# Which engine makes the low halves of the weight tiles between two sublayers

## The reference

```
def swiglu(h, wg, wu, wd):
    return (silu(h @ wg) * (h @ wu)) @ wd
def sandwich_in(h, m, sub, p):
    return rms_norm(h, p['norm_pre'][sub]) * (1 + m[:, 3*sub+1]) + m[:, 3*sub]
def sandwich_out(h, y, m, sub, p, weight):
    return h + weight * m[:, 3*sub+2] * rms_norm(y, p['norm_post'][sub])
def ffn_sub(h, m, sub, j, p):
    y = swiglu(sandwich_in(h, m, sub, p), p['w_gate'][j], p['w_up'][j], p['w_down'][j])
    return sandwich_out(h, y, m, sub, p, 0.5)
```

## Time and profile before

| | us |
|---|---|
| median of the runs | 3351.67 |
| profiled execution, its own time | 3364.72 |
| span of that execution | 3362.2 |
| TensorE busy | 3113.3 (93%) |
| VectorE busy | 1709.3 (51%) |
| ScalarE busy | 1017.1 (30%) |
| GpSimd busy | 281.9 (8%) |
| mean granted TensorE clock | 0.953 |

### The profile page before, as it was taken

One profiled execution on the slowest core, in us unless ns is written; L12 is line 12 of the kernel. 1 busy time (PEld: TensorE's weight loads), 2 busy tenths in 40 slices (PEclk: granted clock), 3 DMA queues, 4 the chain that ended last, 5 costly groups with the idle time before them and its releaser, 6 DMA issues.

```text
span 3362.2 us, 49317 instructions
## 1 busy us (share of the span) xinstructions
PE 3113.3 (93%) x17920; PEld 2858.8 (85%) x17920; DVE 1709.3 (51%) x3019; ACT 1017.1 (30%) x1714; POOL 281.9 (8%) x256
## 2 busy tenths in 40 slices
PE   7999999889898789999999899999988898789998
PEld 3999999879655688999998899999977655689997
DVE  3576565555235754355424666546456337544334
ACT  2312112443424433121123312112343425432223
POOL 2000000410000041000004100000230000310002
PEclk8999999989979899999999899999989899899999
DMA  5343344322100032243323344324331200333333
GB/s 190 111 139 113 113 125 125 103 70 57 53 1 1 1 100 72 60 125 114 99 63 94 93 115 137 112 88 123 106 88 57 60 1 1 92 95 96 94 92 108
DMA packets 454132, 293.19 MB, mean 87 GB/s; under 512 B 25974, under 2 KB 411356, under 8 KB 453980
## 3 DMA queue, kind: packets, MB, share of 16 engines
q1 hardware_dynamic: 453074, 288.02, 29.7%
q10 hardware_dynamic: 906, 3.18, 0.2%
HBM read 289.04 MB, written 2.10 MB: 87 GB/s over the span
## 4 chain that ended last, share of the span: by engine, by line
PE 81%; DVE 9%; issue 4%; ACT 4%; POOL 2%; DMA 0%; ACTq 0%; DVEq 0%; POOLq 0%
PE ps L1639 23%; PE ps L1641 23%; PE ps L1640 23%; PE ps L1976 2%; PE ps L1975 2%; PE ps L2048 2%; PE ps L2001 1%; DVE wsp L1127 1%; DVE hn L1215 1%; POOL scr L700 1%; ACT wsp L766 1%; PE ps L1988 1%; ACT hn L796 1%; DVE ps L1208 1%; PE ps L2033 1%
## 5 line engine op out<-in xcount | busy, mean ns | idle before, releaser
L1639 PE MATMUL ps<-hn,wsp 128*128 128x384 f32 (+1 forms) x3200 | 1059.6, 331 | 56.4 <-DVE hn L1215 34.9
L1640 PE MATMUL ps<-hn,wsp 128*128 128x384 f32 (+1 forms) x3200 | 1047.3, 327 | 0.0
L1641 PE MATMUL ps<-hn,wsp 128*128 128x384 f32 (+1 forms) x3200 | 1046.9, 327 | 0.0
L1127 DVE TENSOR_TENSOR wsp<-raw,wsp 128x1024 fp32r<-128x1024 f32 x376 | 467.4, 1245 | 580.0 <-ACT wsp L766 579.9
L1639 PEld LDWEIGHTS ps<-hn,wsp 128*128 128x128 f32 x3200 | 611.8, 191 | 76.8 <-DVE hn L1215 36.0
L1640 PEld LDWEIGHTS ps<-hn,wsp 128*128 128x128 f32 x3200 | 614.0, 192 | 0.0
L1641 PEld LDWEIGHTS ps<-hn,wsp 128*128 128x128 f32 x3200 | 612.9, 192 | 0.0
L766 ACT ACTIVATE wsp<-raw 128x1024 fp32r<-128x1024 f32 x408 | 428.0, 1051 | 533.7 <-PE ps L1641 533.5
L1639 PE MATMUL ps<-aT,wsp 128*128 128x384 f32 (+1 forms) x1408 | 460.4, 327 | 30.2 <-DVE aT L1306 19.4
L1641 PE MATMUL ps<-aT,wsp 128*128 128x384 f32 (+1 forms) x1408 | 456.3, 324 | 0.0
L1640 PE MATMUL ps<-aT,wsp 128*128 128x384 f32 (+1 forms) x1408 | 456.0, 324 | 0.0
(11 more groups left out here) (205 smaller groups left out, 3099.4 us busy)
## 6 DMA issues: line engine op xcount, KB each, us to landing
modw<-in_w_mod SPq DMA_DIRECT2D x144, 512.0 KB, 4.2
raw<-in_ffn_w_gate SPq DMA_DIRECT2D x192, 256.0 KB, 3.4
raw<-in_ffn_w_up SPq DMA_DIRECT2D x192, 256.0 KB, 4.2
raw<-in_ffn_w_down SPq DMA_DIRECT2D x64, 448.0 KB, 3.4
raw<-in_w_in SPq DMA_DIRECT2D x96, 256.0 KB, 3.1
raw<-in_ffn_w_down SPq DMA_DIRECT2D x64, 256.0 KB, 4.2
raw<-in_w_out SPq DMA_DIRECT2D x64, 256.0 KB, 3.1
raw<-in_ffn_w_down SPq DMA_DIRECT2D x64, 192.0 KB, 3.2
```

Source lines behind the costliest of these rows:

```text
L1127: dve.tensor_tensor(wsp[:, cs, 1, 0:width], raw[:, slot, 0:width], wsp[:, cs, 0, 0:width].bitcast(F32), ALU.subtract).then_inc(wlo_done, 1)
L1639: pe.matmul(dst, w(0), x(0), start=first, stop=False)
L1640: pe.matmul(dst, w(0), x(1), start=False, stop=False)
L1641: return pe.matmul(dst, w(1), x(0), start=False, stop=last)
```

## The change

`split_by_pool` returns False for every tile. So at the ends of the sublayers the low halves of down 1, 3, 6 and 7 and of head 0 and 1 are made by DVE, in `next_lo` of DVE's program, at the place in the step lists that is described above. POOL's `next_lo` never issues anything. The high halves, the loads, the counts of the semaphores and the lists stay as they are; DVE's extra wait on `wlo_done`, which it had behind a low half of POOL, goes.

```
     for l in range(L):
         for sub in range(3):
             i = t - CONV - last_tile0(l, sub) - KD
             if 0 <= i < KD:
-                return i in (1, 3, 6, 7)
+                return False
             i = t - CONV - first_tile0(l, sub)
             if 0 <= i < HEAD:
-                return i < HEAD - 2 and (l, sub) != (0, 0)
+                return False
     return False
```

## The result

The changed kernel took 3391.15 us (median of four runs, 3381.77 to 3393.65), the kernel before 3354.52 beside it: ratio 1.0107, 95% interval 1.0076 to 1.0138. Run once more on another occasion (experiment 4) it had a ratio of 1.0076, interval 1.0049 to 1.0103. So it is slower by some 25 to 37 us. The profiled executions, 3364.72 us before and 3393.65 after, differ by 28.9.

The account below looks back on a forecast made before the run. Taking the order of steps in sublayer boundaries, with VectorE pacing the pre steps, as the limit, it summed 16.6 + 3.7 - 1.3 = 19.0 us, plus 3.5 for the clock: 22.5 us slower, 3374 us; range 3354 to 3392.

Parts of the forecast that it names:

- Tail, down 1 to 5: Down 1 to down 5: ScalarE's squares wait for VectorE instead of GpSimd, ending at the same time; 0 us.
- Pre steps: Down 6 to pre 6: two low halves delay the chain VectorE paces; 2.7 us per boundary of 384.
- the reciprocal: Lead, head 0: VectorE's low half goes ahead of the reciprocal, making it 1.0 us late.
- Lead: Low half of head 1 holds back post 2, 4, 6, so GpSimd's adds start late; 1.45 us per boundary of 384.
- the boundary with halves of 256: Same two low halves in pre steps and lead, but shorter VectorE steps, so its tail wins a little; 3.7 us.
- Last boundary: Sixth boundary, only down 1 and 3: TensorE's waits for GpSimd shrink, post steps hold evacuations; -1.3 of 1.9 us.
- Clock: TensorE idles more in boundaries, so more time at the lower clock; 0.7 us for each of five, 3.5 us.
- Order of steps: All six boundaries before the clock: 16.6 + 3.7 - 1.3 = 19.0 us slower.
- A: Waits for ScalarE hide all but the second pre-step low half; lead loses nothing; 11 us slower, 3362 us; chance 0.24.
- B: GpSimd's chain was the limit, so freeing it speeds tails and lead; 26.5 us faster, 3325 us; chance 0.07.
- C: Clock falls further in five boundaries with TensorE on the path; 17.5 us on top of 19, 3388 us; chance 0.14.
- D: Nothing changes, all moved work lies within waits; 3352 us; chance 0.03.

Follow-up runs that it names:

- experiment 4: The changed kernel run once more, all 32 low halves on VectorE, against the kernel before: ratio 1.0076.
- experiment 1: Kernel before with only the low halves of down 1 and down 3 (12 of 32) moved to VectorE: no difference, interval -7 to +5 us.
- experiment 7: Kernel before with only down 1 and 3's low halves moved to VectorE, placed behind post 0 and post 4: 20.4 us faster.
- number 9: Changed kernel plus unused matrix products filling TensorE's waits before the mean of x half 0 and inside head 0: ratio 1.0024 to the kernel before.
- number 10: Kernel before plus unused matrix products filling its shorter TensorE waits before the mean of x half 0 and inside head 0: 14.5 us faster.
- Experiment 2: Kernel before with only the low halves of down 6 and down 7 (10 of 32) moved to VectorE: +15.2 us.
- experiment 5: Changed kernel with VectorE's low half of head 1 placed behind post 6 instead of ahead of post 2: ratio 1.0046 to the kernel before.
- filled pair: The changed kernel and the kernel before, each with unused products filling TensorE's waits (number 9 and number 10): medians 23.9 us apart.
- Experiment 3: Kernel before with only the low halves of head 0 and head 1 (10 of 32) moved to VectorE: 12.0 us slower.
- the parts: Three runs, each moving one group of low halves in the kernel before: down 1 and 3, down 6 and 7, head 0 and 1; sum 26.7 us.

## Why the prediction was right, and where its size was off

**Tail, down 1 to 5 (taken: 0; the stall changes its releaser).** Right. y0 to x0 moved by +0.7, +0.7, +0.1, +0.5 and, with halves of 256, -0.8 us; experiment 1 shows no difference, and experiment 7 shows what the low half ahead of the post step hides. Of the first +0.7, 0.17 us is there when PE starts the mean (656.41 - 2.13 = 654.28 for 654.11). The low half of down 3 ended at 646.43 - 2.13 = 644.30, near the 644.35 that the prediction gave for waiting out POOL's add in full, and not at its 644.1. The other 0.54 us is the mean itself, 1.41 us for 0.87 at a granted clock of 0.50 for 0.84.

**Pre steps (2.7 us) and the reciprocal (1.0).** Right: 2.79 us in the row above, and at a full clock x0 to y1 is 23.25 us in number 9 for 19.43 in number 10: 3.82, forecast 3.73. Experiment 2 gives +15.2 us for the pre steps of five boundaries. That the next three boundaries show the same rows within a few tenths was not so before the change: x0 to y1 was 21.8 twice, then 22.9 and 20.3.

**Lead (0.45 us behind the reciprocal, 1.45 in all).** The mechanism holds (4.32 us of standing still, experiment 5 takes it back), the size was too small. In the filled pair y1 to x1 is 18.2 us for 17.4 at halves of 384, 0.8 instead of 0.45. The step that was wrong is that with the reciprocal 1.0 us late head 1 would be only 0.5 late, because PE had columns of head 1 in hand. Head 1 came late in full. ACT's high half of head 1 starts 4.90 us behind the reciprocal in number 9 and 4.93 in number 10, and 7.21 us behind it both in the changed kernel and before in the first boundary (in the others of 384 it was 0.35, 0.24 and 0.0 us nearer after the change). What was to cover the delay shows as idle time of PE ahead of the spread, in number 10 and in number 9:

```profile
677.29 0.93 PE L1671 MATMUL ps<-cst,inv 128*128 128x128 f32 x6 [0.35 <-DVE inv L1186]
```

```profile
681.89 0.94 PE L1671 MATMUL ps<-cst,inv 128*128 128x128 f32 x6 [1.36 <-DVE inv L1186]
```

With halves of 256 the stretch grew by 2.2 us, and a second cause is added. The low half waits for ACT, and ACT for PE to end head 1, as the prediction had it, but PE ran head 1 at the lower clock. In the boundary with halves of 256, DVE's post 0 and ACT's high half of head 1, before and after:

```profile
2947.31 0.76 DVE L1234 TENSOR_TENSOR ps<-yM,ps 128x256 f32<-128x256 f32 x2 [0.80 <-PE ps L1671]
```

```profile
2949.85 1.06 ACT L766 ACTIVATE wsp<-raw 128x1024 fp32r<-128x1024 f32 x1 [0.54 <-PE ps L1641]
```

```profile
2976.39 0.76 DVE L1234 TENSOR_TENSOR ps<-yM,ps 128x256 f32<-128x256 f32 x2 [1.31 <-PE ps L1671]
```

```profile
2980.49 1.06 ACT L766 ACTIVATE wsp<-raw 128x1024 fp32r<-128x1024 f32 x1 [2.11 <-PE ps L1641]
```

From the one to the other it was 2.5 us and is 4.1. From the reciprocal to that high half, before and after, PE has the same 28 products, 3.29 us of work and then 5.36, and the granted clock is 1.00 and then 0.57:

```profile
2946.34:2949.85 3.51, 3.29 (x28) 3.29 (x29) 2.71 (x9) 0.81 (x3) 3.03 (x2) 1.00 0.06 15
```

```profile
2974.91:2980.49 5.58, 5.36 (x28) 5.36 (x29) 1.71 (x6) 0.81 (x2) 1.47 (x2) 0.57 0.33 94
```

The filling does not take this back: in number 9 the clock there is 0.66. Experiment 3, +12.0 for 7 to 10, points the same way.

**Last boundary (-1.3).** It won 2.9 us, 2.2 in the trace of number 4 and 2.0 between numbers 10 and 9: the two waits of 0.95 are gone, and the 0.6 taken for evacuations held back by the post steps was not there. Where the up to 1.0 us beyond 1.9 comes from stays open.

**Clock (3.5).** 3.6 by the difference of the filled and the unfilled pairs, and rather more: number 9 was at the lower level for 3.4 us in the fourth boundary in spite of the filling, and took 24.83 us from x0 to y1 there, for 23.25 in the first. In no boundary of number 10 is that so in this stretch.

```profile
2441.27:2466.10 24.83, 21.79 (x112) 19.56 (x111) 15.50 (x38) 9.65 (x22) 4.11 (x5) 0.93 0.26 64
```

That the clock was worth 14.5 us before the change (experiment 10) I had not seen.

**Sum.** Order of steps: forecast 19.0 including the last boundary. The traces of the filled pair have 25.6 - 2.0 = 23.6, the medians of numbers 9 and 10 have 23.9. Of the missing 4.6 us, 1.6 are the lead at halves of 384, 1.6 the fourth boundary as just said, and 1.5 the boundary with halves of 256 (5.2 for 3.7); the last boundary gives 0.7 back, and the rest is spread over small differences. With the clock the forecast was 22.5, and the traces without filling have 29.2 - 2.9 = 26.3. The first comparison's 36.6 us lies above that; the parts (26.7) and the repetition (25.4) lie on it. Why its four runs came out some 10 us higher than the seven of the repetition stays open; the intervals overlap between 1.0076 and 1.0103.

**The rivals.** A fell by experiments 2 and 3, which are slower by themselves. Its price did not follow from its condition either: with one low half of 1.2 us lost per boundary and nothing in the lead, 5 x 1.2 - 1.3 is 4.7 us and not 11. B was wrong about the change, and yet its source was real: 15.8 us lay in POOL's low halves of the tail, and number 7 got them with DVE's behind the post steps. C had the clock falling by 7 us more per boundary, and its price, 19 + 17.5 = 36.5 us, is the 36.6 of the first comparison; by the total alone C would have won, and that the median still lies in the range owes something to luck. Five boundaries did go from 113 to 157 us at the lower level, 8.8 each, but the filled pair shows that only 0.7 of it per boundary, or about 1 with the fourth, lengthened the path beyond the order, for 3.5 in C. D is excluded.

## What to carry to other kernels

Where engines walk through fixed lists, the price of an instruction moved to another engine is what stands behind it there, and behind the wait it brings, until the bounding engine gets its next input: here 0 us or 2.7 us for two instructions of 1.2, and a gain of 3.2 us per boundary when the two of 0 stood one step later. Follow the first piece of work behind the new wait, not the busy share; and if that wait leads back to TensorE, reckon it at the clock that TensorE has there. Count an engine's work as cover for a delay only if that work outlasts the delay: in the lead, with the waits filled, PE was through with it and stood idle for 1.36 us. A stall at the bounding engine is worth removing only if the replacement does not delay the same next input.

## What was not expected of the hardware

- Products without a use, put into TensorE's waits, made the kernel before 14.5 us faster (ratio 0.9957, 0.9939 to 0.9975), with nothing else changed: the granted clock from x0 to y1 rose from 0.81 to 1.00 in the first boundary.
- A low half of VectorE over an add of GpSimd took 1.55 us in the earlier trace rows and 1.71 us three times in the first tail of the changed kernel, for 1.23 alone. This is the row of the second of them:

```profile
644.72 1.71 DVE L1127 TENSOR_TENSOR wsp<-raw,wsp 128x1024 fp32r<-128x1024 f32 x1 [1.08 <-ACT wsp L766]
```

The best version run (12) keeps down 6, 7 and head 0, 1 on GpSimd, has down 1 and 3 on VectorE behind their post steps and fills TensorE's waits: 3323.31 us beside 3353.77, 0.9% faster than the kernel before.
